# Rolling TensorE's feed-forward loop: five written-out passes become one hardware loop of 864 matmuls

## The reference

```
up = hn @ w_up                                  # 1024 -> 2 * 2816
full = concat([buf, up])
conv = sum(full[:, j:j + T] * conv_w[j] for j in range(3)) + conv_b
a, gt = split(conv, 2)
f = (a * silu(gt)) @ w_down                     # 2816 -> 1024
x = x + f;  y = rmsnorm(x)
```

## Time and profile before

| | us |
|---|---|
| median of 3 runs | 2328.18 (2326.68 to 2328.29) |
| the profiled execution: its own time | 2328.29 |
| the profiled execution: span of its instructions | 2326.5 |
| PE busy in the span | 2234.8 |

### The profile page before, as it was taken

One profiled execution on the slowest core, in us unless ns is written; L12 is line 12 of the kernel. 1 busy time (PEld: TensorE's weight loads), 2 busy tenths in 40 slices (PEclk: granted clock), 3 DMA queues, 4 the chain that ended last, 5 costly groups with the idle time before them and its releaser, 6 DMA issues.

```text
span 2326.5 us, 34317 instructions
## 1 busy us (share of the span) xinstructions
PE 2234.8 (96%) x14736; PEld 2173.0 (93%) x14736; DVE 1156.3 (50%) x1278; ACT 604.5 (26%) x747; POOL 280.0 (12%) x432
## 2 busy tenths in 40 slices
PE   5799999999999999999999999999999999999995
PEld 5699989899989999999999988999999999999995
DVE  4715535344444344324654233447566655656665
ACT  4423234223422322233322134221111111111112
POOL 5989800000000000000000000000000000000000
PEclk9899999999989999999999999999999999999997
DMA  6311114112322222225422143111111111111111
GB/s 238 109 46 45 48 49 164 65 69 87 127 107 73 83 85 73 110 96 204 136 83 81 45 172 146 45 49 55 46 46 46 46 46 46 47 54 46 46 40 73
DMA packets 45181, 190.23 MB, mean 82 GB/s; under 512 B 5104, under 2 KB 5168, under 8 KB 41456
## 3 DMA queue, kind: packets, MB, share of 16 engines
q1 hardware_dynamic: 32400, 118.18, 14.7%
q0 software_dynamic: 10784, 53.36, 6.1%
q10 hardware_dynamic: 1872, 16.83, 1.8%
HBM read 152.59 MB, written 35.93 MB: 81 GB/s over the span
## 4 chain that ended last, share of the span: by engine, by line
PE 88%; DVE 4%; issue 4%; ACT 2%; POOL 1%; DMA 1%; DVEq 0%; ACTq 0%; POOLq 0%
PE ps L256 25%; PE ps L257 24%; PE ps L259 24%; PE ps L1774 1%; PE ps L2118 1%; PE ps L2094 1%; DVE T L869 1%; DVE GT L411 1%; PE ps L2128 1%; POOL W L672 1%; PE ps L1750 0%; ACT TMP L402 0%; DVE XR L2480 0%; DVE WL L250 0%; DVE XR L2485 0%
## 5 line engine op out<-in xcount | busy, mean ns | idle before, releaser
L256 PE MATMUL ps<-XH,WH 128*128 128x344 f32 x1704 | 550.1, 326 | 6.1 <-ACT STAGE L311 2.5
L257 PE MATMUL ps<-XL,WH 128*128 128x344 f32 x1512 | 481.1, 321 | 0.0
L256 PE MATMUL ps<-XN,WH 128*128 128x344 f32 x1248 | 398.6, 321 | 0.2 <-DVE WL L250 0.2
L257 PE MATMUL ps<-XN,WH 128*128 128x344 f32 x1248 | 396.9, 321 | 0.0
L250 DVE TENSOR_TENSOR WL<-WRAW,WH 128x1024 fp32r<-128x1024 f32 x177 | 225.0, 1272 | 298.0 <-ACT WH L245 297.0
L259 PE MATMUL ps<-XH,WL 128*128 128x344 f32 x1704 | 362.4, 321 | 0.0
L256 PEld LDWEIGHTS ps<-XH,WH 128*128 128x128 f32 x1704 | 322.5, 189 | 17.4 <-issue 11.8
L245 ACT ACTIVATE WH<-WRAW 128x1024 fp32r<-128x1024 f32 x177 | 186.5, 1054 | 522.9 <-PE ps L259 508.8
L257 PEld LDWEIGHTS ps<-XL,WH 128*128 128x128 f32 x1512 | 286.6, 190 | 0.1
L259 PEld LDWEIGHTS ps<-XH,WL 128*128 128x128 f32 x1704 | 286.5, 189 | 0.0
L259 PE MATMUL ps<-XN,WL 128*128 128x344 f32 x1248 | 264.1, 319 | 0.0
(11 more groups left out here) (522 smaller groups left out, 3126.3 us busy)
## 6 DMA issues: line engine op xcount, KB each, us to landing
WRAW<-in_wslabs SPq DMA_DIRECT2D x177, 512.0 KB, 3.5
scratch_spill<-STAGE SPq DMA_DIRECT2D x40, 516.0 KB, 2.7
ZS<-scratch_spill POOLq DMA_DIRECT2D x24, 516.0 KB, 5.7
XIN<-in_xT POOLq DMA_DIRECT2D x1, 4128.0 KB, 18.2
XR<-in_xT ACTq DMA_DIRECT2D x2, 2064.0 KB, 8.7
out_y<-XR SPq DMA_DIRECT2D x8, 516.0 KB, 3.0
CACHES<-in_ck ACTq DMA_DIRECT2D x4, 1024.0 KB, 14.1
CACHES<-in_cv ACTq DMA_DIRECT2D x4, 1024.0 KB, 16.6
```

The source lines that it names most:

```text
L256: pe.matmul(out[t], WH[:, slot, w, :], xh(k, t), start=(k == 0), stop=False)
L257: pe.matmul(out[t], WH[:, slot, w, :], xl(k, t), start=False, stop=False)
```

## The change

The Python `for` over the five passes on PE becomes a hardware loop. The body is issued once, the counter `i` is a register, and the thresholds of the waits in `up` and `down` (`i * 12 + ...` for `w_lo`, `i * 12 + ...` for `acc_free`, `i * 4 + ...` for `f_lo`) are computed in registers. A compare-and-branch closes each pass. The matmuls, their order and what they wait for are the same; ACT, DVE, POOL and SP are not touched.

```
             pe_entry(pe, SL_FFN, G_FFN, 3, 5)
             up(0, SL_FFN, G_FFN, 0, 0, 2)
-            for i in range((NF // 2 - 1) // 2):
+            with pe.Fori(0, (NF // 2 - 1) // 2) as i:
                 for c in range(2):
                     n, g = SL_FFN + 4 + 6 * c, G_FFN + 4 + 12 * c
                     up(i, n, g, 12, 24)
```

## The result

The changed kernel takes 2352.96 us (median of 4 runs, 2348.65 to 2354.97), the kernel before 2327.43 us: a ratio of 1.0109, 95% interval 1.0094 to 1.0126. It is slower by 25 us. The forecast was 2338, slower by 10, and even its own range for a head that is fetched at each jump ended at 2345. The direction and the cause hold; the size does not.

The account below looks back on a forecast made before the run. PE alone was taken to bound the kernel. Four jumps at 2.1 us stall plus 0.4 us clock add 10 us to 2328.29, giving 2338 us; a fetched head ranged 2331.5 to 2345, and the overall range reached down to 2327.2.

Parts of the forecast that it names:

- a head that is fetched at each jump: Likelier case at the loop's four jumps back: 2331.5 to 2345 us, chance 0.55.
- PE alone sets the stretch: In the five passes PE is busy throughout and waits for nobody; additions to its stream are paid unless its queue covers them.
- the register operations are covered: Some 40 register operations a pass and the branch cost nothing behind queued matmuls; uncovered they would be 9 us.
- The rival on register operations: Wait chains in the loop outlast PE's queue: 20 groups x 5 passes x 0.03 us = 3 us, 2331; chance 0.03.
- How far the sequencer runs ahead: At a wait of line 2314, 1.36 us or about 8 matmuls lie queued, and this is subtracted from each stall.
- The head is gone by the time of the jump: At a pass's end PE jumps back seven blocks; the body's first code is likely gone and must be fetched; chance 0.55.
- the rival: Body kept: PE's code memory holds eight blocks, so the 6.9-block body stays unless it touches eight; 2328.2 us, chance 0.40.
- The price of a stall: Each of four jumps waits for one fetch: 2.1 us, between 0.8 and 4.3, the high end behind a weight slab.
- The clock: A halt at a jump may lower PE's clock afterwards: 0.4 us a jump taken, between 0 and 1.7.
- What q8 would show: PE's code queue falls from 103 packets by 24 or less, or stays near 103 if all blocks come again; 75 if wrong.
- The rival that fewer fetches help: With the body kept, 28 code packets fewer make room for weight slabs: 0 to 0.5 us gained; measurably faster, chance 0.02.

Follow-up runs that it names:

- e1: Changed kernel with the loop's first instruction placed at slot 0 of a 256-instruction fetch block: 2326.89 us, ratio 0.9998 to the kernel before.
- e3: Changed kernel plus a prefetch hint for the closing branch as first instruction of each pass, head not placed: 2327.13 us, ratio 1.0000 to the kernel before.
- e4: Changed kernel with half the body, nested loops of five and two over single chunks: 2328.17 us, ratio 1.0009 to the kernel before.
- e5: Changed kernel with the loop head placed at slot 24 of a fetch block: 2329.09 us, ratio 1.0002 to the kernel before.
- e6: Changed kernel with the loop head at slot 32, four instructions in an eighth block: 2333.06 us, ratio 1.0015 to the kernel before.
- e9: Changed kernel with the loop head at slot 36, eight instructions in an eighth block: 2324.67 us in one execution, kernel before 2329.42.
- e11: Changed kernel with both the prefetch hint and the loop head at slot 64: 2326.30 us in one execution, kernel before 2329.42.
- e2: Changed kernel with the loop head placed at slot 64 of a fetch block: 2332.55 us, ratio 1.0027 to the kernel before.
- e8: The changed kernel itself, unaltered, measured again beside the others: 2354.14 us, ratio 1.0113 to the kernel before.
- e10: Changed kernel with the loop head at slot 48, 20 instructions in an eighth block: 2328.17 us in one execution, kernel before 2329.42.
- e7: Changed kernel with the loop head at slot 239, 17 instructions before the block's edge: 2342.22 us, ratio 1.0054 to the kernel before.

## Why the prediction was right and wrong, step by step

- **PE alone sets the stretch, and the register operations are covered.** Right. Without a halt the loop takes 681.9 us in e1, e3, e4, e5, e6, e9 and e11, as in the kernel before. (The rival on register operations counts 20 groups with waits a pass; there are 2 x (4 + 8) = 24, so it would have come to 3.6 us instead of 3.)
- **How far the sequencer runs ahead.** Wrong in size, on the kind side: 1.36 us was read at a wait where the sequencer had itself been held back: it stands at 1723.1, and DVE was emptying the banks for it up to 1721.82 + 1.23 = 1723.05. At the branch 17 matmuls, 2.56 us, were still to start.

```profile
1721.82 1.23 DVE L2451 TENSOR_TENSOR XR<-XR,ps 128x1032 f32<-128x1032 f32 x1 [0.18 <-PE ps L259]
```

- **The head is gone by the time of the jump.** Right in the outcome, for half of a reason. I took it from the longest return seen. The memory holds eight blocks, which the rival had: the body of 6.9 blocks stays if it touches seven of them (e1, e5), and also if it touches eight and the ninth isn't read before the jump (e6, e9, e11). In the change it touches eight, since the head lies in the last slot, and the ninth, read ahead and never used, pushes out the first. The rival even named that condition, with 24 instructions to spare (28 by the count of 1764); I had no row that said where the head lies, and gave the chances without it.
- **The price of a stall: the step that failed.** The step was that a jump waits for one fetch, at 2.1 us. One fetch is 3.3 to 3.8 us from the branch to the next instruction (my 3.0 + 0.2 was low) and leaves 1.1 with 2.56 queued (e2), half of my term, since the queue covers more. But the change pays two in series: the head is alone in its block, the block behind it was dropped too, and reading ahead has no time. 3.5 + 3.4 - 2.56 = 4.3 us. Two blocks in a row was nowhere in my sum, though its high end of 4.3, for a fetch behind a slab, happens to be the same number. No slab's transfer was needed for it.
- **The clock.** Taken at 0.4 a jump from two halts of 1.2 us. Measured 2.1: the halts were about 4 us long and each was followed by a fall, for up to 6.8 us where I had 3.4 as the most. The trace before had longer halts to read it from (the one of 3.24 us under e8). Both errors go with the second fetch: 4 x (4.1 + 2.1) = 25 where I had 4 x (2.1 + 0.4) = 10.
- **What q8 would show.** Wrong. I expected one packet a jump for the head, 79 or more but below 103, and near 103 only if all blocks came again. It is 9 a pass and 112 in all: after a miss all eight blocks that the body touches come again, and the ninth is read ahead.
- **The rival that fewer fetches help.** e1, with 27 packets fewer, is at 0.9998 (0.9989 to 1.0008): nothing.

The Trainium skill gives TensorE 128 KiB for instructions, 2048 of them, in blocks of 256 ("Runtime: NRT & Kernel Launch", section "Instruction fetch mechanics"). The runs agree: eight blocks of 16 KB, seven of the body and the one read ahead in e1, eight of the body in e6, e9 and e11. The same section says that a taken branch whose target isn't in the current two-page window stalls; e1 and e5 jump back over six blocks in 0.2 us, so for TensorE the measurement decides against the figure of two. That a branch out of the memory waits for a fetch is borne out, with 3.3 to 3.8 us.

What stays open: why a miss drops the following blocks as well, what sets the moment at which the ninth block is asked for, and where exactly between 20 and 36 instructions behind the edge every jump misses. That the clock can fall behind a halt without any fetch is shown by the trace before; what length of halt it takes was not tried.

## What to carry to other kernels

A hardware loop whose body nearly fills the instruction memory is free or costs microseconds a pass depending on where the body happens to begin; any instruction added ahead of it can decide it, so place the head or hint the closing branch, and here both gave back all of the 25 us. Count the blocks that the body touches and one more for the read-ahead (up to eight in all was safe here), and look at the compare-and-branch records and at the packets of the instruction queue: 0.2 or 3.4 us tell the case at once. When pricing a stall on a bound engine, ask what the next instruction needs as well, and what the halt does to the clock; each can be worth as much as the stall.

## What the runs showed of the hardware that I had not expected

- The block behind the loop's last one isn't always read before the jump: with 4 and 8 instructions in the eighth block (e6, e9) at none of four jumps, with 20 at one of four (e10), with 36 at all four (e2). The delay from entering a block to its request isn't fixed (e9, e10); that a jump cancels the request fits, but isn't shown.
- With the head at slot 64 a jump cost 1.1 us and no clock; with it at the edge 4.1 us and 3.4 to 6.8 us at half clock. 17 instructions between the two fetches (e7) brought the 25 us down to 13.8.
- The hint costs 31 ns a pass, and saves by not fetching.
